# Interleaved instead of halved: which 128-row blocks make a quarter of w_down in a seven-product block multiply

## The chip, the cores and the metric

The kernel runs on one core of a Trainium2 chip. The metric is the device time of one execution in microseconds. The kernel before takes 941.87 us (median of 3 runs, 941.16 to 942.93).

## The reference, cut to what matters

One layer of a streaming encoder over 544 output tokens (512 prompt and 32 sample frames) with a model width of 1024. The change touches only the MLP at its end:

```python
def _mlp(x, g, w_up, w_down):          # w_up 1024 x 4096, w_down 4096 x 1024
    h = _rmsnorm(x, g)
    return jnp.square(jax.nn.relu(h @ w_up)) @ w_down
```

All is float32. The result must agree with float32 accuracy, so the kernel splits each operand into a rounded high part and the low rest and makes three matrix products of them (high x high, high x low, low x high).

## The kernel before, in words

Everything is done on one core with five engine programs written out by hand: SyncE loads weights, ScalarE (ACT) rounds them to the high part, GpSimd (POOL) makes the low part, TensorE (PE) multiplies, VectorE (DVE) and ACT empty the results. Order comes from each engine's own program order and from semaphores alone.

The hidden width of 4096 is taken in four rounds of 1024 (`rr`). In a round the kernel first makes eight tiles u[f], f = 0 to 7, of 128 hidden channels x 544 tokens ("up", PE line 659): tile f comes from one 512 KB block of 128 columns of w_up, loaded into one of the four slots of `w_raw`. Slot and order are those of `load_group` and of the loop at lines 512 to 521. Then the round's part of `@ w_down` is done. In the last round that is a plain multiply. In the first three (`rr < N_SEVEN`) it is a multiply of 2 x 2 blocks with seven products in place of eight (Winograd's form of Strassen's scheme, `seven`, PE line 981): for each of four pairs `p` of output tiles (`P_` = 4 rr + p, 12 in all) the 1024 x 256 piece of w_down is cut into quarters A11, A12, A21, A22. The first index is the output tile of the pair (a slot of `w_raw`), the second is one half of the 1024 hidden channels, which must be the same half of u that the forms B11, B21 and so on hold. Four sums of quarters (S1 to S4, `wsum_pair`, DVE line 1825) are made in `gate_c`.

Each of seven forms (A11, S1, A12, S2, S4, S3, A22, in this order on PE) is then made ready by these steps:

- ACT copies it, rounded, into its place in `w_hi` (line 1383). This waits until the product of the pair before that used the same place is done (`seven_free`).
- For the five forms in `BY_DMA` (A11, A12, A22 straight from `w_raw`; S4, S3 from `gate_c`) ACT also writes the negated rounded value into `w_lo` (line 1385), and POOL issues a DMA that adds the raw form onto it (line 635, `accum_op=ALU.add`). For S1 and S2 DVE subtracts (line 1842).
- PE waits for the low part (`low_made`), then makes 12 matmuls for the form.

A quarter is read through `quarter` (line 350). `w_raw[:, slot]` holds 8 blocks k of 128 values in each partition, one for each 128 hidden channels. Before the change a quarter's half h is the blocks 4h to 4h+3, one run of 512 values (2 KB) in a partition. To make it so that B11 and B21 pair channels m and m + 4, the tiles of w_up come in the order 0, 4, 1, 5, 2, 6, 3, 7.

The slots of `w_raw` are used again and again: a load of w_down for pair P_ (line 531) waits in `seven_left` until the low parts of pair P_ - 2 in that slot have landed and its sums are made; in pairs 2 and 3 of a round the next round's w_up loads (line 521) come behind the same wait.

Of the kernel before, what the change touches and what calls it, by code (L numbers as in the profile page):

```python
# [42 lines left out]
N_SEVEN = ROUNDS - 1  # L43
N_GROUPS = (3 + ROUNDS + 1) * GROUPS_PER_STAGE
PAIRS = KC // 2
# [43 lines left out]
def build(nc, x_prompt, x_sample, cache_k, cache_v, cache_conv, meta, g_mix, w_in, w_dw, b_dw,  # L89
# [5 lines left out]
    def weight(w, name):  # L95

        return w.rearrange("(k p) (n c) -> p k n c", p=P, c=P)
# [4 lines left out]
    wup_v = weight(w_up[0], "up")  # L102
# [12 lines left out]
    with ExitStack() as ctx:  # L115
        def sb(name, shape, dt=F32, where=ctx):
            return where.enter_context(nc.sbuf_tensor(name, shape, dt))

        def sem(name):
            return ctx.enter_context(nc.semaphore(name))  # L120


        w_raw = sb("w_raw", [P, RING, KC, P])
# [127 lines left out]
        raw_post = [sem(f"raw_post{n}") for n in range(4)]  # L251
# [64 lines left out]
        def lows_of_post(g, n):  # L316
            return RING * (g - 2) + n + 1
# [20 lines left out]
        def low_made(engine, P_, name):  # L338
            engine.wait_ge(wform_lo[MADE[name] - 1], (16 if name in BY_DMA else 1) * (P_ + 1))

        MADE = {w: n + 1 for n, (w, _, _, _) in enumerate(SEVEN)}

        ADDED = {"x11": 1, "z11": 2, "x12": 3, "y12": 4, "w12": 5, "x22": 6, "x21": 7, "y22": 8, "z21": 9}
# [6 lines left out]
        def quarter(P_, name):  # L350

            slot = 2 * (P_ % 2) + (name[1] == "2")
            h = int(name[2]) - 1
            return w_raw[:, slot, h * PAIRS:(h + 1) * PAIRS, :]

        def wsum(name):
            at = OUTTOK + SUM_FORMS.index(name) * PAIRS * P
# [2 lines left out]
        def raw_form(P_, name):  # L360
            return wsum(name) if name in SUM_FORMS else quarter(P_, name)
# [13 lines left out]
        def up_group(rr):  # L375
            return 3 * GROUPS_PER_STAGE + GROUPS_PER_STAGE * rr
# [32 lines left out]
        def x_half(t, h):  # L409
            (_, col, n), = X_COLS[t]  # L410
            return xT[:, h * KC // 2:(h + 1) * KC // 2, col:col + n]
# [5 lines left out]
        def _(sync):  # L417
# [70 lines left out]
            def load_group(g, view):  # L488
                for n in range(4):
                    sync.wait_ge(lo_post, lows_of_post(g - 1, n))  # L490
                    sync.dma_start(w_raw[:, n], view(n)).then_inc(raw_post[n], 16)
# [10 lines left out]
            def seven_left(P_, b):  # L502

                for name in ("A11", "A12") if b == 0 else ("A22",):
                    low_made(sync, P_, name)
                sync.wait_ge(wsum_done, len(SUM_FORMS) * (P_ + 1))

            for rr in range(ROUNDS):
                g0 = up_group(rr)
                if rr == 0:  # L510
                    with sync.Fori(0, 2) as j:
                        load_group(g0 + j, lambda n: wup_v[:, :, bass.ds(2 * j + n // 2 + PAIRS * (n % 2), 1), :].rearrange("p k n c -> p k (n c)"))
                else:
                    for j in range(2):
                        for n in range(4):
                            if j == 0:
                                seven_left(PAIRS * (rr - 1) + 2 + n // 2, n % 2)
                            sync.wait_ge(lo_post, lows_of_post(g0 + j - 1, n))

                            f = 4 * j + n if rr == N_SEVEN else 2 * j + n // 2 + PAIRS * (n % 2)  # L520
                            sync.dma_start(w_raw[:, n], wup_v[:, :, 8 * rr + f, :]).then_inc(raw_post[n], 16)
                if rr < N_SEVEN:
                    for p in range(PAIRS):
                        P_ = PAIRS * rr + p
                        for b in range(2):
                            slot = 2 * (p % 2) + b
                            if p < 2:
                                sync.wait_ge(lo_post, lows_of_post(g0 + 1, slot))
                            else:
                                seven_left(P_ - 2, b)  # L530
                            sync.dma_start(w_raw[:, slot], wdown_v[:, rr, :, 2 * p + b, :]).then_inc(raw_seven[slot], 16)
                else:
                    with sync.Fori(0, 2) as j:
                        load_group(g0 + 2 + j, lambda n: wdown_v[:, rr, :, bass.ds(4 * j + n, 1), :].rearrange("p k n c -> p k (n c)"))
# [115 lines left out]
        def _(pe):  # L650
# [63 lines left out]
            def scores(i, hh, first=False):  # L714
# [47 lines left out]
                for j in (2, 3):  # L762
                    bank, off, _, q0 = KT[j]
                    mm = score_split(bank, off, j, q0)
# [735 lines left out]
        def _(dve):  # L1500
# [313 lines left out]
            def wsum_pair(P_, name):  # L1814
                if name == "S1":
                    for slot in range(2 * (P_ % 2), 2 * (P_ % 2) + 2):
                        dve.wait_ge(raw_seven[slot], 16 * (P_ // 2 + 1))
                if P_:

                    low_made(dve, P_ - 1, name)  # L1820
                if name in ("S2", "S4"):
                    dve.wait_ge(wsum_done, len(SUM_FORMS) * P_ + SUM_FORMS.index(name))
                a, b, op = {"S1": (quarter(P_, "A21"), quarter(P_, "A22"), ALU.add), "S2": (wsum("S1"), quarter(P_, "A11"), ALU.subtract),
                            "S4": (quarter(P_, "A12"), wsum("S2"), ALU.subtract), "S3": (quarter(P_, "A11"), quarter(P_, "A21"), ALU.subtract)}[name]
                nc.vector.tensor_tensor(wsum(name), a, b, op).then_inc(wsum_done, 1)  # L1825
# [169 lines left out]
```

## Time and profile before

| | |
|---|---|
| median of 3 runs | 941.87 us |
| the profiled execution | 942.93 us |
| its span in the profile | 941.2 us |
| PE busy | 925.9 us (98%) |
| DVE, ACT, POOL busy | 648.1, 600.3, 250.5 us |
| mean granted TensorE clock | 0.996 |
| queue 0 (DMAs issued by POOL) | 16272 packets, 43.52 MB, 26.1% of 16 engines |
| queue 1 (DMAs issued by SP) | 176666 packets, 80.28 MB, 31.6% of 16 engines |

The span is the time between the first and the last instruction in the profile; the 1.7 us beside it are outside. Shares of DMA queues are the time that their packets took as a share of 16 engines' span, so the two can add up to a little more than 1 in a full stretch. "To landing" is the time from a DMA's issue to its semaphore.

### The profile page before, as it was taken

What the parts mean: (1) busy time and instruction counts of PE and PEld (TensorE: products, weight loads), DVE (VectorE), ACT (ScalarE), POOL (GpSimd) and SP (SyncE); (2) the same over time, 40 slices, a digit from 0 to 9 for tenths busy, and PEclk for the clock granted to TensorE, in tenths of its full rate; (3) what the DMA queues carried; (4) which work ended last, traced back from release to release, by engine and by line L of the source; (5) the groups of instructions that cost most, each with busy time, mean ns of one, the idle gap of its engine ahead of it and who ended that gap; (6) DMA issues with size and microseconds to landing.
All of it is one profiled execution on the core that took longest, in us unless ns stands there. A gap on an engine that the chain in (4) does not pass through costs nothing.

```text
span 941.2 us, 19528 instructions
## 1 busy us (share of the span) xinstructions
PE 925.9 (98%) x7329; PEld 906.3 (96%) x7329; DVE 648.1 (69%) x1181; ACT 600.3 (64%) x1004; POOL 250.5 (27%) x224
## 2 busy tenths in 40 slices
PE   8999999999999999999999999999999999999997
PEld 8999999999999999999999999989999999999997
DVE  6579999999999999998653335863587358622233
ACT  6787887878787878776833345663466356623353
POOL 5311010101010110102243444334433532444440
PEclk9999999999999999999999999999999999999998
DMA  7777667675758584859133232598259735963202
GB/s 183 159 171 135 172 126 178 119 183 108 180 113 187 104 199 98 173 133 211 46 112 90 85 85 78 120 211 186 68 119 224 172 89 113 230 155 88 87 23 96
DMA packets 198172, 127.25 MB, mean 135 GB/s; under 512 B 36397, under 2 KB 182237, under 8 KB 198122
## 3 DMA queue, kind: packets, MB, share of 16 engines
q1 hardware_dynamic: 176666, 80.28, 31.6%
q0 software_dynamic: 16272, 43.52, 26.1%
q10 hardware_dynamic: 5184, 2.78, 1.0%
q8 instruction: 32, 0.52, 0.2%
q14 instruction: 18, 0.15, 0.0%
HBM read 75.97 MB, written 7.06 MB: 88 GB/s over the span
## 4 chain that ended last, share of the span: by engine, by line
PE 84%; DVE 5%; ACT 4%; DMA 4%; SPq 1%; issue 1%; ACTq 0%; DVEq 0%
PE dense L659 61%; PE z L981 6%; PE dense L981 5%; PE z L779 3%; DMA w_lo<-w_raw 3%; PE dense L953 3%; PE z L743 2%; PE z L813 2%; DVE gate_c L1825 1%; ACT w_hi L1383 1%; DVE part L1782 1%; DVE acc L1559 1%; DMA w_raw<-in_w_in_dram 1%; ACT w_lo L1385 1%; ACT n L1346 1%
## 5 line engine op out<-in xcount | busy, mean ns | idle before, releaser
L659 PE MATMUL dense<-r_hi,w_hi 128*128 128x272 f32 (+1 forms) x1008 | 210.7, 291 | 1.4 <-ACT r_hi L1116 0.7
L659 PE MATMUL dense<-r_lo,w_hi 128*128 128x272 f32 (+1 forms) x1008 | 209.6, 289 | 0.0
L659 PE MATMUL dense<-r_hi,w_lo 128*128 128x272 f32 (+1 forms) x1008 | 209.5, 289 | 0.0
L630 POOL TENSOR_TENSOR w_lo<-w_raw,w_hi 128x1024 fp32r<-128x1024 f32 x56 | 134.8, 2410 | 196.9 <-ACT w_hi L1070 196.9
L1559 DVE SCALAR_TENSOR_TENSOR acc<-conv_in,cw_cur,acc 128x574 f32<-128x574 f32 x232 | 172.8, 811 | 0.5
L659 PEld LDWEIGHTS dense<-r_hi,w_hi 128*128 128x128 f32 x1008 | 158.2, 188 | 1.9 <-issue 0.9
L659 PEld LDWEIGHTS dense<-r_lo,w_hi 128*128 128x128 f32 x1008 | 158.7, 188 | 0.6 <-DVE r_lo L1540 0.6
L659 PEld LDWEIGHTS dense<-r_hi,w_lo 128*128 128x128 f32 x1008 | 159.0, 188 | 0.0
L607 POOL DMA_DIRECT2D w_lo<-w_raw x53 | 45.1, 851 | 361.9 <-ACT w_lo L1072 361.9
L1070 ACT ACTIVATE w_hi<-w_raw 128x1024 fp32r<-128x1024 f32 x110 | 115.7, 1052 | 34.1 <-PE z L981 21.6
L659 PE MATMUL dense<-s_hi,w_hi 128*128 128x272 f32 x640 | 132.2, 288 | 0.0
L659 PE MATMUL dense<-s_hi,w_lo 128*128 128x272 f32 x640 | 131.6, 288 | 0.0
L659 PE MATMUL dense<-s_lo,w_hi 128*128 128x272 f32 x640 | 131.4, 287 | 0.0
L659 PEld LDWEIGHTS dense<-s_lo,w_hi 128*128 128x128 f32 x640 | 100.0, 188 | 0.0
L659 PEld LDWEIGHTS dense<-s_hi,w_hi 128*128 128x128 f32 x640 | 99.7, 188 | 0.1
L659 PEld LDWEIGHTS dense<-s_hi,w_lo 128*128 128x128 f32 x640 | 99.7, 188 | 0.0
L1346 ACT ACTIVATE n<-n 128x544 f32<-128x544 f32 x32 | 21.1, 658 | 88.0 <-DVE n L1787 88.0
L1787 DVE SCALAR_TENSOR_TENSOR n<-dense,rstd 128x544 f32<-128x544 f32 x32 | 23.1, 723 | 69.2 <-PE dense L659 64.3
L1072 ACT ACTIVATE w_lo<-w_raw 128x1024 fp32r<-128x1024 f32 x53 | 55.6, 1050 | 0.0
L635 POOL DMA_DIRECT2D w_lo<-w_raw x36 | 30.6, 850 | 63.6 <-ACT w_lo L1385 62.7
L1383 ACT ACTIVATE w_hi<-gate_c 128x512 fp32r<-128x512 f32 x48 | 29.9, 629 | 16.9 <-DVE gate_c L1825 8.1
L1837 DVE TENSOR_TENSOR xT<-z,xT 128x272 f32<-128x272 f32 x48 | 19.8, 438 | 23.7 <-PE z L981 23.5
(305 smaller groups left out, 1941.9 us busy)
## 6 DMA issues: line engine op xcount, KB each, us to landing
w_raw<-in_w_in_dram SPq DMA_DIRECT2D x54, 512.0 KB, 5.7
w_lo<-w_raw POOLq DMA_DIRECT2D x53, 512.0 KB, 5.0
w_raw<-in_w_up_dram SPq DMA_DIRECT2D x32, 512.0 KB, 4.4
w_raw<-in_w_down_dram SPq DMA_DIRECT2D x32, 512.0 KB, 3.9
w_lo<-w_raw POOLq DMA_DIRECT2D x36, 256.0 KB, 5.6
w_lo<-gate_c POOLq DMA_DIRECT2D x24, 256.0 KB, 5.7
w_raw<-in_w_pw_dram SPq DMA_DIRECT2D x8, 512.0 KB, 3.9
w_raw<-in_w_out_dram SPq DMA_DIRECT2D x8, 512.0 KB, 3.9
```

What stands on the lines that cost most here:

```text
L607: pool.dma_start(w_lo[:, s].bitcast(F32), w_raw[:, s], accum_op=ALU.add).then_inc(lo_done[s], 16)
L630: pool.tensor_tensor(w_lo[:, n], w_raw[:, n], w_hi[:, n].bitcast(F32), ALU.subtract).then_inc(lo_post, 1)
L635: pool.dma_start(form_place(w_lo, name).bitcast(F32), raw_form(P_, name), accum_op=ALU.add).then_inc(wform_lo[MADE[name] - 1], 16)
L659: mm = nc.tensor.matmul(out[:, h, 0:half], w[:, wslot, k, :], m[:, k, c0 + h * half:c0 + (h + 1) * half], start=(k == 0 and n == 0), stop= ...
L779: mm = nc.tensor.matmul(z[:, dst[0], dst[1]:dst[1] + n], m[:], part_[src], start=False, stop=False, skip_group_check=True)
L953: mm = nc.tensor.matmul(part_out(n, p), w[:, n, k, :], m[:, k, cols], start=(k == 0 and j == 0), stop=(k == KC - 1 and j == 2))
L981: mm = nc.tensor.matmul(product_bank(P_, b), w[:, m, :], u_form(moving, m, low), start=(begin and m == 0 and j == 0), stop=(m == PAIRS - 1 ...
L1070: done = nc.scalar.activation(w_hi[:, s], w_raw[:, s], ACT.Copy)
L1072: done = nc.scalar.activation(w_lo[:, s], w_raw[:, s], ACT.Copy, scale=-1.0)
L1346: nc.scalar.activation(n32[:, n % 2, 0:OUTTOK], n32[:, n % 2, 0:OUTTOK], ACT.Square).then_inc(u32_done, 1)
L1383: mm = nc.scalar.activation(form_place(w_hi, name), raw_form(P_, name), ACT.Copy)
L1559: nc.vector.scalar_tensor_tensor(dst, src, w, dst, ALU.mult, ALU.add).then_inc(tap_done, 1)
```

## The change

```diff
         def quarter(P_, name):
 
             slot = 2 * (P_ % 2) + (name[1] == "2")
-            h = int(name[2]) - 1
-            return w_raw[:, slot, h * PAIRS:(h + 1) * PAIRS, :]
+            return w_raw[:, slot].rearrange("p (k t) c -> p t k c", t=2)[:, int(name[2]) - 1]
...
                 if rr == 0:
                     with sync.Fori(0, 2) as j:
-                        load_group(g0 + j, lambda n: wup_v[:, :, bass.ds(2 * j + n // 2 + PAIRS * (n % 2), 1), :].rearrange("p k n c -> p k (n c)"))
+                        load_group(g0 + j, lambda n: wup_v[:, :, bass.ds(4 * j + n, 1), :].rearrange("p k n c -> p k (n c)"))
...
-
-                            f = 4 * j + n if rr == N_SEVEN else 2 * j + n // 2 + PAIRS * (n % 2)
-                            sync.dma_start(w_raw[:, n], wup_v[:, :, 8 * rr + f, :]).then_inc(raw_post[n], 16)
+                            sync.dma_start(w_raw[:, n], wup_v[:, :, 8 * rr + 4 * j + n, :]).then_inc(raw_post[n], 16)
```

The tiles of w_up are now loaded in their natural order in every round, so that tiles 2m and 2m + 1 are a pair. A quarter of w_down is therefore every second block of 128 values: blocks 0, 2, 4, 6 for the first half and 1, 3, 5, 7 for the second. In a partition that is four runs of 512 bytes with gaps of 512 bytes in place of one run of 2 KB. The places in `w_hi` and `w_lo` and the sums in `gate_c` keep their layout. No instruction, wait or semaphore is added or taken away.

## Rows read from the trace of the kernel before

**Rows 1.** The page, busy time and share of TensorE.
```profile
PE 925.9 (98%) x7329; PEld 906.3 (96%) x7329; DVE 648.1 (69%) x1181; ACT 600.3 (64%) x1004; POOL 250.5 (27%) x224
```
**Rows 2.** Waits of PE: who for whom, us in total, times, longest.
```profile
PE dense L981 <- DMA w_lo<-w_raw: 4.2, 4, 2.2
...
PE dense L981 <- DVE xT L1835: 0.6, 1, 0.6
```
**Rows 3.** Windows: busy us of each engine, granted clock, DMA share, GB/s.
```profile
609.50:628.50 19.00, 16.80 (x121) 16.59 (x121) 12.79 (x28) 12.13 (x22) 7.74 (x10) 0.91 0.93 188
703.50:720.00 16.50, 15.37 (x119) 14.78 (x118) 13.03 (x28) 12.35 (x23) 8.09 (x10) 1.00 1.00 192
795.50:812.00 16.50, 15.30 (x118) 14.70 (x116) 12.90 (x28) 12.31 (x23) 8.19 (x10) 1.00 1.00 193
```
**Rows 4.** Chain of waits, first round: start us, us, what.
```profile
609.57 4.95 DMA w_lo<-w_raw
614.57 2.28 PE dense L981 x12
616.85 11.56 PE z L981 x84
628.41 10.54 PE dense L981 x84
```
**Rows 5.** Chain of waits, third round.
```profile
795.48 3.32 DMA w_lo<-w_raw
...
798.84 1.77 PE dense L981 x12
800.61 1.75 PE z L981 x12
...
803.89 8.11 DMA w_lo<-w_raw
...
812.13 10.78 PE dense L981 x84
```
**Rows 6.** Low-part DMAs of line 635: time to landing.
```profile
DMA to landing us min/median/max: 3.2/5.7/8.1
```
**Rows 7.** Groups by line: names, shapes, count, busy us, mean ns.
```profile
L1787 DVE SCALAR_TENSOR_TENSOR n<-dense,rstd 128x544 f32<-128x544 f32 x32 | 23.1, 723 | 69.2 <-PE dense L659 64.3 <-ACT rstd L1112 4.8
L1825 DVE TENSOR_TENSOR gate_c<-w_raw 128x512 f32<-128x512 f32 x24 | 16.5, 687 | 7.8 <-DMA w_raw<-in_w_down_dram 7.8
L1133 ACT ACTIVATE gate_a<-dense 128x544 f32<-128x544 f32 x8 | 5.0, 625 | 16.0 <-PE dense L659 16.0
L1383 ACT ACTIVATE w_hi<-w_raw 128x512 fp32r<-128x512 f32 x36 | 22.4, 623 | 10.7 <-PE dense L981 7.1 <-PE z L981 3.6
```
**Rows 8.** The page, POOL's own time for issuing a low-part DMA.
```profile
L607 POOL DMA_DIRECT2D w_lo<-w_raw x53 | 45.1, 851 | 361.9 <-ACT w_lo L1072 361.9
...
L635 POOL DMA_DIRECT2D w_lo<-w_raw x36 | 30.6, 850 | 63.6 <-ACT w_lo L1385 62.7
```
**Rows 9.** DMA queue of POOL, 785 to 788.5 us: packets, MB, share of 16 engines.
```profile
q0 software_dynamic: 144, 0.26, 43.5%
```
**Rows 10.** DMA queue of POOL, 100 to 200 us (rows of 4 KB).
```profile
q0 software_dynamic: 1788, 6.54, 36.1%
```
**Rows 11.** DMA queue of SP, 445 to 478 us (loads in pieces of 512 bytes).
```profile
q1 hardware_dynamic: 4981, 2.52, 26.6%
```
**Rows 12.** DMA queue of SP, 925 to 941 us (stores of 2 and 4 KB rows).
```profile
q1 hardware_dynamic: 768, 1.97, 33.6%
```
**Rows 13.** DMA queues and issues of POOL, 795.5 to 812 us.
```profile
q0 software_dynamic: 1131, 2.06, 76.3%
...
w_lo<-w_raw POOLq DMA_DIRECT2D x6, 256.0 KB, 5.5
```
**Rows 14.** Loads of w_up, issue to landing: 840 to 880, then 530 to 580.
```profile
w_raw<-in_w_up_dram SPq DMA_DIRECT2D x1, 512.0 KB, 4.2
...
w_raw<-in_w_up_dram SPq DMA_DIRECT2D x7, 512.0 KB, 4.0
```

## The prediction
> **What bounds the kernel now.** I read first the page's list of busy engines, then PE's waits, then the stretches with the seven products, then the DMA queues in them. PE is busy 98% of the span [rows 1], so a change pays or costs only through PE's gaps or clock. The reader should see three things. First, the touched stage has few gaps, nearly all of one kind: PE waits 4.2 us in four places for a low part built by DMA, and 0.6 us in a fifth place where the named DVE operation is not what came late [rows 2]. Second, the place of each gap is in the chain. In the first round the DMA for A22 of pair 0 is issued at 609.57 and takes 4.95 us, and PE starts again at 614.57; after this gap of 2.2 us the granted clock falls: 12 matmuls take 2.28 us and the next 84 take 11.56, where 84 take 10.54 elsewhere [rows 4, 5], and the window around has a mean clock of 0.91 [rows 3]. In the third round the same DMA takes 3.32 us and the gap is small, but the DMA for A11 of pair 2, issued at 803.89, takes 8.11 us and PE waits for it: pair 1 began at 800.61 and lasts 10.54, pair 2 begins at 812.13, some 0.9 us late [rows 5]. Third, why 8.11 us: from 795.5 to 812 the 16 DMA engines are full (share 1.00), as in the same stretch a round earlier, 703.5 to 720 [rows 3]. POOL's queue has 76% of it [rows 13]. So the low-part DMAs sit on PE's path in two ways: by their own length at pair 0, and by the queue's total at pair 2. This is where the change works.
>
> **The change part by part.** *Order of the w_up loads.* 24 loads are renamed among themselves, each still 1024 pieces of 512 bytes into the same slot behind the same waits. A load in natural order (last round) lands in 4.2 us, seven in the old order in 4.0 [rows 14]. Bound: 0.2 us either way on a load that PE doesn't wait for. I take 0.
>
> *DVE and ACT reading a quarter with gaps.* 48 sums on DVE and 72 copies on ACT now read four runs of 128 values. The nearest rows with more than one run are reads of two runs of 272: on DVE 723 ns for 544 columns against 687 for 512 (1.33 and 1.34 ns a column), on ACT 625 ns for 544 against 623 for 512 [rows 7]. So runs cost nothing that can be seen; I take 0. Both engines are idle a third of the span, but ACT's two copies of A22 stand on the path at pair 0; if each cost 20 ns more, three rounds would lose 0.1 us.
>
> *POOL's issue.* 36 of the 60 low-part DMAs read `w_raw`; these go from 128 rows of 2 KB to 512 pieces of 512 bytes on the reading side. POOL spends 850 ns on a DMA of 128 rows, whether of 4 KB or 2 KB [rows 8]. Both rows have 128 rows, so they don't say what four times as many pieces cost: from 0 to 3 x 0.85 = 2.55 us. I take 0, as the bytes at least cost nothing, and keep 2.55 for the range.
>
> *The DMA itself.* This is the term that counts. In a quiet stretch one 256 KB low-part DMA shows 144 packets, 128 rows and 16 for the semaphore, and 43.5% of 16 engines x 3.5 us = 24.4 us, which is 190 ns a row of 2 KB if the semaphore costs nothing [rows 9]. With 4 KB rows the same kind of DMA shows 6.54 MB = 1597 rows in 36.1% x 16 x 100 = 578 us, 362 ns a row [rows 10]. The slope is 172 ns for 2 KB, so of the 190 ns some 18 are fixed. A piece of 512 bytes is then 172/4 + 18 = 61 ns, four of them 244: 54 ns more for each old row, 128 rows over 16 engines are 8 on each, **+0.43 us per DMA**. Plain copies support a fixed part: 512-byte pieces take 26.6% x 16 x 33 / 4981 = 28 ns [rows 11], while SP's stores of 1.97 MB in 672 rows (768 packets less 16 for each of six DMAs) take 33.6% x 16 x 16 / 672 = 128 ns for 2930 bytes [rows 12]; that is 41 ns per 1000 bytes and 7 ns fixed. The bounds are wide. Below: if the fixed 18 ns belong to the semaphore packets, splitting is free, 0. Above: a piece may have a floor that longer rows hide; it can be as long as a whole row, 190 ns, which gives 4 x 190 - 190 = 570 ns a row and +4.6 us per DMA. I take 0.43 because slope and copies both point near it.
>
> The Trainium skill, page "DMA: Bandwidth & Descriptors", section "Why small descriptors are slow (HBM only)", says that transfers from SBUF to SBUF don't suffer from small descriptors, and its specification table puts the least size for full rate at 512 bytes, just what the pieces now have. By this rule the sum would be 0; the traces so far neither confirm nor refute it for an accumulating DMA.
>
> *From the DMA to PE.* At pair 0 PE stands behind A22's DMA in each of three rounds: 3 x 0.43 = 1.3 us, and in the first round A11's DMA of pair 1 runs beside it, another 0.4. In the full stretch up to A11 of pair 2, POOL issues six DMAs from `w_raw` [rows 13]; five (A22 of pair 0, A11, A12, A22 of pair 1, A11 of pair 2) must be through before PE goes on. With the engines full, five times 0.43 = 2.15 us are added to the gap, in rounds two and three: 4.3 us. In the first round pair 2 begins at 628.41 with no gap behind the 11.56 us of pair 1 [rows 4], so I count nothing. Other forms have a cushion: a form is rebuilt when its product has ended, so its DMA has 10.54 - 1.51 (own product) - 1.25 (two ACT copies) - 0.3 (hand-over) = 7.5 us [rows 4, 7] against a median of 5.7 [rows 6]; the queue is still full there, so I count 0.5 us for each of rounds two and three, 1.0. Then the clock: the gap before pair 2 grows from 0.9 to about 3 us, longer than the 2.2 us after which the clock fell in the first round, where it cost 0.5 (2.28 against 1.77) + 1.0 (11.56 against 10.54) = 1.5 us [rows 4, 5]. I count it for one of the two rounds. Sum: 1.3 + 0.4 + 4.3 + 1.0 + 1.5 = **8.5 us**. The profiled execution, 942.93 us (span 941.2 and 1.7 outside), becomes 951.4; it is the slowest of three, and on the median of 941.87 the same sum gives 950.4. I say 951.
>
> **The rivals.** *Splitting is free.* The cost is proportional to bytes, or the added time falls into cushions. For it: 18 ns is a small difference of two large numbers. Against it: the copies' 7 ns, and full engines where PE waits. It gives 0 to 1.9 us more, 942 to 943.8. It decides if a piece takes under some 48 ns. The rule of the Trainium skill cited above would have it so.
>
> *A floor under each piece.* The accumulate reads two streams and writes one, and what two long rows show need not hold for short ones; or POOL needs its time per piece. At 100 ns a piece a DMA gains 4 x 100 - 190 = 210 ns x 8 = 1.7 us. The stretch of pairs 1 to 3 is full already, so nearly all of it goes to PE: some 11 DMAs from `w_raw` a round x 1.7 less 2 us of cushion = 17 a round, 51 in all, 993 us. At 190 ns it would be 11 x 4.6 x 3 = 150 us, 1093. If POOL were to take 3.4 us an issue, a pair would need 3 x 3.4 + 2 x 0.85 = 11.9 us of it against 10.54 of PE, about +25 us, 967. Against a strong floor: 18 ns of fixed time at 2 KB leaves room only for one wholly hidden under the bytes.
>
> *Faster.* The load queue gets its turn between shorter packets: against a 61 ns piece in place of a 190 ns row, the loads of w_down in the full stretch (DVE waits 7.8 us for them [rows 7]) land sooner, forms are made sooner, and A11 of pair 2 lands in under 7.2 us in place of 8.11. At most PE's gaps of 4.8 us [rows 2] and the clock's 1.5 go: 942.9 - 6.3 = 936.6. Against it: A11 of pair 2 is issued late because PE's product before it ends at 802.36 [rows 5], not because a load is late, and less of the full engines for POOL's queue makes it later. It decides only if the pieces take no more engine time than the rows.
>
> **How the numbers follow.** The forecast (slower by 3 to 15 us) gets 0.50, free splitting 0.20, a floor 0.22, faster 0.08. A measurement of this kernel can't tell less than 0.2% (1.9 us) from no change. So faster 0.08, same 0.20, slower 0.72. The range runs from 941.5, which leaves out the faster case, to 985, which takes in a floor of up to about 95 ns a piece and leaves out the rest (0.12).
>
> **What would show it.** Right: in the profile after, POOL's queue has 36 x 384 = 13824 more packets with the same bytes, and in the quiet stretch one DMA from `w_raw` takes some 31 us of engine time in place of 24.4 and lands at 3.6 in place of 3.2 [rows 6, 9], while DMAs from `gate_c` keep theirs. The wait before pair 2 in rounds two and three is 2 to 3 us, with the clock below 1 behind it once or twice. DVE's 687 and ACT's 623 ns stay. Wrong: packets that don't grow in number (the pieces are joined), a piece clearly over 61 ns or at 48, POOL's 850 ns grown, or gaps of PE at other places, above all one before every product of pairs 1 to 3.

## The result, and the profile after

The changed kernel takes **950.87 us** (median of 4 runs, 949.6 to 952.47) against 942.4 us for the kernel before on the same chip (4 runs, 941.16 to 943.25). The ratio is **1.0092 [1.0072, 1.0112]**: 8.5 us slower. The profiled execution of the changed kernel is 950.32 us with a span of 948.6 us.

The page, busy time of the engines of the kernel after:

```profile
PE 928.7 (98%) x7329; PEld 907.5 (96%) x7329; DVE 648.1 (68%) x1181; ACT 600.2 (63%) x1004; POOL 266.2 (28%) x224
```

DVE and ACT have not moved by more than 0.1 us [rows 1]: their reads with gaps cost nothing. POOL has 15.7 us more. The groups by line (names, shapes, count, busy us, mean ns, idle before) say where; 1323 ns stand against 850 [rows 8], 686 against 687 and 623 against 623 [rows 7]:

```profile
L632 POOL DMA_DIRECT2D w_lo<-w_raw x36 | 46.1, 1323 | 60.7 <-ACT w_lo L1382 45.9 <-ACT w_hi L1380 14.3 <-issue 0.4
L1380 ACT ACTIVATE w_hi<-w_raw 128x512 fp32r<-128x512 f32 x36 | 22.4, 623 | 11.9 <-PE dense L978 6.7 <-PE z L978 5.1
L1822 DVE TENSOR_TENSOR gate_c<-w_raw 128x512 f32<-128x512 f32 x24 | 16.5, 686 | 11.0 <-DMA w_raw<-in_w_down_dram 11.0
```

(Lines of the kernel after are 3 lower than before: 632 for 635, 1380 for 1383, 978 for 981.) The waits of PE from 560 to 860 us, in the columns of [rows 2]:

```profile
PE dense L978 <- DMA w_lo<-w_raw: 3.4, 2, 2.2
PE z L978 <- DMA w_lo<-w_raw: 2.4, 4, 1.0
PE z L978 <- DVE xT L1834: 2.0, 3, 0.7
PE dense L978 <- DMA w_lo<-gate_c: 1.3, 2, 1.2
```

The sum goes from 4.8 us in five places to 9.1 us in eleven, and a kind is there that was not: PE waits for DVE's additions into xT at line 1834 (the 0.6 us of [rows 2] name another line). None of the eleven stands at the start of pair 2. POOL's DMA queue (q0) in two stretches: first a quiet one (693 to 699 us, which holds one cut DMA), and then in the full stretch of the third round (799.5 to 816.5 us): packets, MB, share of 16 engines.

```profile
q0 software_dynamic: 528, 0.26, 39.4%
...
q0 software_dynamic: 2640, 1.70, 79.7%
```

One cut DMA shows 528 packets, 512 pieces and 16 more, and 0.394 x 16 x 6 = 37.8 us of engine time where a whole one had 24.4 [rows 9]: 106 ns more for each old row, 0.85 us more on each engine. In the whole kernel q0 has 30096 packets for the same 43.52 MB, 13824 more. All 60 DMAs of the line take 4.1/6.5/8.4 us to landing (min/median/max) in place of 3.2/5.7/8.1 [rows 6].

The same two full stretches as windows (columns of [rows 3]):

```profile
704.00:721.00 17.00, 14.38 (x108) 13.56 (x108) 11.46 (x24) 11.52 (x21) 9.51 (x9) 1.00 1.09 173
799.50:816.50 17.00, 13.89 (x97) 13.20 (x95) 9.85 (x21) 10.22 (x19) 9.07 (x8) 0.90 1.04 163
```

The engines stay full (share over 1) but move 173 and 163 GB/s where they moved 192 and 193: more time for the same bytes. And in the third round the clock is 0.90 where it was 1.00.

The chain of waits in the third round shows which way the time reaches PE (start us, us, what):

```profile
800.20 4.38 DMA w_lo<-w_raw
...
804.60 8.25 DMA w_raw<-in_w_down_dram
...
812.93 0.70 DVE gate_c L1822
...
813.72 0.70 DVE gate_c L1822
...
814.94 0.43 DVE xT L1834
815.37 0.60 DVE gate_c L1822
815.97 0.36 DVE xT L1834
816.33 0.14 issue
816.47 3.25 PE z L978 x24
```

In the kernel before, the chain went from one low-part DMA to the next [rows 5]. Now it goes round the ring of slots: A22 of pair 0 lands and frees its slot of `w_raw`, the load of w_down for pair 2 goes into it and takes 8.25 us, DVE can then make the sums of pair 2, and in DVE's program these stand ahead of the additions of pair 1 that PE waits for.

Round by round (the first from its first product to the next up stage, the second and third from up stage to up stage) the two profiles give 46.2 and 46.0 us, 91.9 and 94.9, 92.1 and 95.3: -0.1, +3.0 and +3.2 us. The spans differ by 7.4 us; the other 1.3 us lie ahead of the touched stage. The -0.1 hides something: the clock fell in the first round of the profile before [rows 3, 4] and not in that of the kernel after. In e1 below, whose DMAs have whole rows as before and whose clock stayed at 1.00 there, the rounds take 44.9, 92.0 and 92.0 us. Against it the changed kernel loses 1.2, 3.0 and 3.3 us, 7.4 in all. That the median grew by 8.5 is not fully placed by these single executions.

### The profile page after: what moved, and what is told of

Read it like the earlier page. It is cut to its first block, busy times and chain, and to the rows that moved or that the text cites. A ratio compares the mean times of both kernels' runs of the same rounds, so it can differ in the third digit from the quotient of the medians.

```text
span 948.6 us, 19528 instructions
## 1 busy us (share of the span) xinstructions
PE 928.7 (98%) x7329; PEld 907.5 (96%) x7329; DVE 648.1 (68%) x1181; ACT 600.2 (63%) x1004; POOL 266.2 (28%) x224
## 3 DMA queue, kind: packets, MB, share of 16 engines
q0 software_dynamic: 30096, 43.52, 28.4%
## 4 chain that ended last, share of the span: by engine, by line
PE 80%; DMA 7%; DVE 6%; ACT 4%; issue 1%; SPq 1%; POOL 0%; DVEq 0%; ACTq 0%
PE dense L656 61%; PE z L978 4%; PE z L776 3%; DMA w_lo<-w_raw 3%; PE dense L978 3%; PE dense L950 3%; DMA w_raw<-in_w_down_dram 2%; PE z L740 2%; PE z L810 2%; DVE gate_c L1822 2%; ACT w_hi L1380 1%; DVE part L1779 1%; DVE acc L1556 1%; DMA x_tok<-in_x_sample_dram 1%; DMA w_raw<-in_w_in_dram 1%
## 5 line engine op out<-in xcount | busy, mean ns | idle before, releaser
L604 POOL DMA_DIRECT2D w_lo<-w_raw x53 | 45.1, 852 | 361.9 <-ACT w_lo L1069 361.9
L632 POOL DMA_DIRECT2D w_lo<-w_raw x36 | 46.1, 1323 | 60.7 <-ACT w_lo L1382 45.9
```

Of the source, the lines that this page charges most:

```text
L604: pool.dma_start(w_lo[:, s].bitcast(F32), w_raw[:, s], accum_op=ALU.add).then_inc(lo_done[s], 16)
L632: pool.dma_start(form_place(w_lo, name).bitcast(F32), raw_form(P_, name), accum_op=ALU.add).then_inc(wform_lo[MADE[name] - 1], 16)
```

## The experiments

Each ran beside the kernel before; ratios are to it, with their 95% interval. Diffs are cut: `...` marks lines left out, and where a DMA's `.then_inc(...)` is the same on both sides it is left out too. In e1, e4, e5 and e7 the forms hold other values than the reference's, so these serve for time alone. The medians of before were 942.43 us (e1, e4, e6, e7), 942.17 (e5, e8, e9, e10), 942.84 (e11 to e13) and 942.86 (e14).

**e1: all but the DMAs' rows.** The kernel after, with the source of the 36 DMAs one run of 2 KB.

```diff
-                    pool.dma_start(form_place(w_lo, name).bitcast(F32), raw_form(P_, name), accum_op=ALU.add)
+                    # raw: blocks 4h to 4h+3 for A11, A12, A22
+                    pool.dma_start(form_place(w_lo, name).bitcast(F32), raw, accum_op=ALU.add)
```

> The changed kernel, but the 36 low-part DMAs read the first or second 2 KB of the slot in one run, as before, and not the four interleaved runs; the low parts of A11, A12 and A22 are therefore those of other blocks and the output isn't the reference's. DVE and ACT still read four runs, w_up still comes in natural order. Theory (all of the 8.5 us comes from the cut rows of these DMAs): 942.4, ratio 1.000 within 0.002, POOL's issue back at 0.85 us and queue 0 back at 16272 packets. Rival (order of the loads, or DVE and ACT reading with gaps, costs something): clearly above, up to 950.9.

Measured: 942.63 us, 1.0002 [0.9992, 1.0012]. The whole cost is in the cut rows of these DMAs. The order of the w_up loads and the reads with gaps on DVE and ACT cost nothing that can be seen (together 1.1 us at most). POOL's issue is back at 851 ns.

**e4: only A22 of pair 0 whole** (3 of the 36 DMAs, the others cut).

```diff
+                    if name == "A22" and P_ % PAIRS == 0:
+                        h = int(name[2]) - 1
+                        raw = w_raw[:, 2 * (P_ % 2) + (name[1] == "2"), h * PAIRS:(h + 1) * PAIRS, :]
```

> The changed kernel, but the DMA for A22 of pair 0 (3 of the 36) reads one run of 2 KB per partition; its low part is that of other blocks. The quiet cut DMA takes about 0.85 us more engine time and 0.43 us more of POOL. Theory Q (full DMA engines: only total work counts): each round loses one of five or six additions, 0.85 x 2 rounds = 1.7 us, so about 949. Theory L (latency at pair 0: PE and the load ring of w_raw stand behind this one DMA): the whole of 3 x 1.3 us and more goes, 945 to 947.

Measured: 948.32 us, 1.0069 [1.0049, 1.0089]. Three whole DMAs give back 2.6 us, with an interval that reaches zero (1.0069 against 1.0092, each within 0.0020); the 33 others alone cost 5.9, with 4.6 to 8.4 by the interval of the ratio. Theory Q's 949 lies nearer than theory L's 945 to 947.

**e5: only A22 of pair 0 cut** (these 3, the 33 others whole; the diff is against e4).

```diff
-                    if name == "A22" and P_ % PAIRS == 0:
+                    if name not in SUM_FORMS and not (name == "A22" and P_ % PAIRS == 0):
```

> The complement of e4: the changed kernel, with cut rows only in the DMA for A22 of pair 0 (3 of 36); the other 33 DMAs from w_raw read one run of 2 KB, so their low parts are those of other blocks. Theory L (PE and the slot behind it wait for this one landing, 0.9 us later): +2.5 us against before, 944.9, so that e4 and e5 add up to the whole change. Theory Q (only work in the full queue counts): +0.85 in two rounds, 944.1 at most, and nothing in the first.

Measured: 948.04 us, 1.0054 [1.004, 1.0068]. Both theories (944.9 and 944.1) are passed. Three cut DMAs cost 5.9 us by the medians and 3.8 to 6.4 by the interval of the ratio, more than their own 3 x 0.85. So a cut DMA has no fixed price: these three cost more than 1.2 us each, the 33 of e4 under 0.3. That the two parts don't add up (5.9 and 5.9 against 8.5) is likely but not shown, since the interval of their sum overlaps that of the whole. The chain of e5 in the first round:

```profile
610.07 4.35 DMA w_lo<-w_raw
614.42 0.02 issue
614.43 9.23 DMA w_raw<-in_w_down_dram
623.66 0.03 DVEq L339
623.70 0.04 issue
623.74 0.70 DVE gate_c L1826
...
627.28 4.78 PE z L982 x24
```

It is the same ring. The load starts when A22 has landed and takes 9.23 us, where the kernel before has 6.6 for a load that starts at the same time (614.5). Why is not shown: in e5's second and third rounds the load behind A22 takes 5.5 us, less than the 5.7 of the kernel before. There the cut DMA itself is what costs: it lands in 4.22 us where 3.3 had been enough, and PE's gap is 1.5 us in place of 0.6.

A second thing makes the first round dear, the clock. The first round of the kernel before and of e5, as windows (columns of [rows 3]):

```profile
602.00:650.00 48.00, 45.80 (x353) 45.59 (x352) 30.35 (x65) 29.21 (x52) 20.09 (x20) 0.96 0.90 189
602.00:650.00 48.00, 43.65 (x323) 43.25 (x322) 28.10 (x60) 28.39 (x51) 17.45 (x19) 0.93 0.88 176
```

In e5 the clock falls twice, to 0.83 on average from 614.4 to 623.7 us, behind a gap of 2.24 us, and to 0.64 from 627.3 to 632.1, behind one of 2.10 us: the 24 matmuls of the chain's last line take 4.78 us where they take 3.24 otherwise. From busy time and clock I estimate 3.3 us for both falls, against 1.5 in the kernel before. So of the 3.8 us that e5's first round is longer, about half is waits and half is clock. The profiled execution is also the slowest of e5 (949.53 us; the fastest took 945.27).

**e6: POOL later, nothing cut.** The kernel before, with a small memset on POOL ahead of each of the 36 DMAs, about as long as the 0.43 us that a cut DMA adds to its issue.

```diff
+                    if name not in SUM_FORMS:
+                        pool.wait_ge(idled, idles)
+                        pool.memset(idle_col[:], 0.0).then_inc(idled, 1)
                     pool.dma_start(form_place(w_lo, name).bitcast(F32), raw_form(P_, name), accum_op=ALU.add)
```

> The kernel before, with a memset of 128x384 on POOL (about 0.42 us) ahead of each of the 36 DMAs that read w_raw, so that these are issued as much later as the changed kernel's are; rows stay whole. If issue time on POOL is an equal part of the 8.5 us: +3 to 4 us, 946. If the engine time of the pieces is what costs: at most the 3 x 0.4 us at pair 0, 943.7 or less, since full engines make the later issue invisible.

Measured: 943.12 us, 1.0007 [0.9997, 1.0018], at most 1.7 us, as the second theory had it. The memset takes 419 ns (median). The longer issue alone explains little.

**e7: two runs of 1 KB in place of four of 512 bytes.** The kernel before, with quarters of two blocks by turns (the halves of u keep their order, so the sums pair other channels than the reference has).

```diff
-            return w_raw[:, slot, h * PAIRS:(h + 1) * PAIRS, :]
+            return w_raw[:, slot].rearrange("p (a t b) c -> p t a b c", a=2, t=2)[:, h]
```

> The kernel before, with quarters that are interleaved by two blocks (blocks 0, 1, 4, 5 and 2, 3, 6, 7): two runs of 1 KB in a partition. The order of w_up stays that of before, so pairs of channels don't fit and the output isn't the reference's. With a fixed 31 ns per piece (from 296 ns for four pieces): 234 ns a row, +0.35 us engine time per DMA, POOL +0.14 us. If the cost is linear in pieces: a third of 8.5, 945.2. If cushions swallow the first part of it: 943 to 944.

Measured: 947.05 us, 1.0047 [1.0032, 1.0062]. Its queue in the quiet stretch from 693 to 699 us, then the durations of POOL's issues (min/median/max ns) in e7 and, below, in the kernel after:

```profile
q0 software_dynamic: 272, 0.26, 30.3%
...
L635 POOL DMA_DIRECT2D w_lo<-w_raw x36: 1182/1195/1721, 591.7 to 828.8; - x36
```

```profile
L632 POOL DMA_DIRECT2D w_lo<-w_raw x36: 1261/1276/1822, 592.5 to 832.1; - x36
```

0.303 x 16 x 6 = 29.1 us of engine time, 227 ns for each 2 KB row. With 190 for one run and 296 for four, a run more costs some 35 ns. So the engine time grows by the run, while POOL's issue makes a step for the first cut (848 to 1195 ns) and little after it (1276). The time of the kernel (+4.6 us for one more run a row, +8.5 for three) lies between the two laws and proves neither.

**e8 and e9: A22's low part by a subtraction on POOL**, with no DMA, in the kernel before (e8) and after (e9).

```diff
+                    if name in BY_POOL:          # ("A22",)
+                        pool.tensor_tensor(form_place(w_lo, name), raw_form(P_, name), form_place(w_hi, name).bitcast(F32), ALU.subtract)
+                        continue
```

> The kernel before, with the low part of A22 made by a subtraction on POOL in all 12 pairs (128x512, about 1.2 us by half of line 630's 2.4) in place of ACT's negated copy and the DMA. If the waits for these DMAs are what PE's gaps in the three rounds are made of, the gaps at pair 0 (2.2, 0.6, 0.6), the 1.5 us of clock behind the first and the 0.9 us before pair 2 in two rounds go: 936 to 937. Rival: POOL's reads slow DVE beside them (the 2.8 us of one sum beside a subtraction of POOL), and the gain is lost: 940 to 943.

> The changed kernel with the same edit as e8. Theory (the interleaved quarter is dear only for the DMA, at 35 ns of engine time per extra run, and only where the queue is full or PE stands behind): 24 cut DMAs are left, none at pair 0's A22 and four in the full stretch; most of the 8.5 us goes, 937 to 940. If the cost were spread over all 36 alike: a third goes, plus what e8 gains.

Measured: e8 944.57 us, 1.0027 [1.0018, 1.0036]; e9 943.87 us, 1.0022 [1.0012, 1.0032]. The expected gain of e8 is not there, and it is above the rival's 940 to 943 too; e9 meets neither of its numbers (937 to 940, or two thirds of the 8.5 us left). Its waits and its chain show a gap that moved to the first product of pair 1:

```profile
PE z L985 <- DMA w_lo<-w_raw: 6.3, 3, 2.2
```

```profile
608.81 1.58 POOL w_lo L637
610.39 5.43 DMA w_lo<-w_raw
615.82 0.04 issue
615.87 10.80 PE z L985 x84
```

POOL is busy for 1.58 us with the subtraction and issues A11 of pair 1 later, for which PE waits next. What counts is the comparison of the two: with twelve DMAs fewer the cut rows of the other 24 seem to cost nothing (e9 is not slower than e8). But both stand about 2 us at the start of pair 1 in every round, and that common gap can hide a cost; e14 looks behind it.

**e10: A11, A12 and A22 all on POOL**, in the kernel before.

```diff
-        BY_POOL = ("A22",)
+        BY_POOL = ("A11", "A12", "A22")
```

> The kernel before, with the low parts of A11, A12 and A22 all made by POOL's subtraction; of the DMAs only the 24 from gate_c are left. No form from w_raw touches a DMA, so the interleaving would cost nothing here. PE's gaps should be gone as in e8: 935 to 937. Rival: three subtractions of 1.2 us a pair beside DVE's work slow DVE, which then holds PE: 940 or more.

Measured: 951.48 us, 1.0095 [1.008, 1.011]. The expected gain turned into a loss. DVE's sums of e10, by line (in the kernel before these two groups have means of 687 and 1222 ns):

```profile
L1829 DVE TENSOR_TENSOR gate_c<-w_raw 128x512 f32<-128x512 f32 x24 | 24.7, 1030 | 0.0
L1829 DVE TENSOR_TENSOR gate_c<-gate_c,w_raw 128x512 f32<-128x512 f32 x12 | 17.4, 1448 | 0.9
```

The sums of the first group take 1030 ns on average here, the longest 3.42 us, with the subtractions of POOL beside them. (The kernel before has single sums of 2.8 us in its second group.) DVE is late with its additions, and PE waits for them (5.8 us in three places).

**e11: A22 of pair 0 two microseconds earlier**, in the kernel before. ACT makes it in the gap before T3 of the last tile of u; the place in `w_hi` is free by then.

```diff
                         for name in ("T2", "T3", "T4"):
+                            if name == "T3" and f == KC - 1:
+                                form_high(PAIRS * rr, "A22")
                             u_sum_high(rr, m, name)
...
-                    form_high(P_, "A22")
```

> The kernel before, but ACT makes the high and negated copy of A22 of pair 0 before the sum T3 of the last tile of u, in place of after T4, so POOL can issue its DMA some 2 us earlier (607.4 in place of 609.6 in the first round). Nothing else moves; the number of DMAs and their rows stay. Theory (the landing of A22 of pair 0 is what costs at pair 0, and the load of w_down behind it): PE's gaps there (2.2, 0.6, 0.6 us) and the 1.5 us of lower clock in the first round go, 942.2 - 4.9 = 937.3 us. Rival (the work only waits at the next place, as when POOL did the subtraction, 944.6): 941 to 943 us.

Measured: **937.8 us, 0.9956 [0.9943, 0.9969]**, expected 937.3. By the medians that is 5.0 us less than before, by the ratio 4.1 (2.9 to 5.4). It beats both kernels. Of PE's 4.8 us of waits 1.5 are left, none at pair 0:

```profile
PE z L981 <- DMA w_lo<-w_raw: 1.5, 2, 0.9
```

**e12: the same edit in the kernel after.**

> The kernel after, with the same edit: A22 of pair 0 is made some 2 us earlier; all 36 DMAs still read four runs a row. Theory (the ring: A22's landing, then the load of w_down for pair 2 into its slot, then DVE's sums, then PE): an earlier landing pulls the whole ring forward, so most of the 8.5 us go, 943 to 945 us (943.9 was measured with A22 made by POOL without a DMA). Rival (the cost is in the sheer engine time of the 33 other DMAs, in the full stretch): only the gap at pair 0 goes, 948 us.

Measured: 946.58 us, 1.0047 [1.0028, 1.0065]. The edit gives 4.3 us here too, but the cost of the cut rows stays: 946.58 against 937.8 is 8.8 us. So a late A22 of pair 0 is not the cause of the 8.5 us; the theory asked for 943 to 945, the rival for 948, and the interval (945.5 to 949.0) holds the rival's number alone. The chain of e12 in the second round:

```profile
709.44 8.23 DMA w_lo<-w_raw
717.69 8.54 DMA w_raw<-in_w_down_dram
726.31 0.70 DVE gate_c L1823
727.10 0.63 DVE gate_c L1823
729.84 3.24 PE dense L978 x24
```

The ring is there again, one pair further on: low part of pair 1, load of pair 3, DVE's sums, PE in pair 2. Both transfers in it run among full engines. Whichever pair it enters by, the ring has two long transfers, and among cut rows both are longer. The load behind A22 of pair 0 takes 6.6, 5.7 and 5.7 us in the three rounds before, 5.5, 5.7 and 5.7 in e1, and 7.1, 7.3 and 8.2 in the kernel after.

**e13: DVE's sums later.** The kernel after, with pair 1 taking pair 0's order on DVE: x12 stands behind one sum of the late load, not behind three operations on it.

```diff
-                if p > 0:
+                if p > 1:
                     made(P_, "A11")
...
                 else:
+                    if p:
+                        made(P_, "A11")
+                        add_product(P_, "x11")
                     following("S1")
...
-                if p == 0:
+                if p <= 1:
                     following("S2")
```

> The kernel after, but in pair 1 of a round DVE takes its steps in the order of pair 0: the additions of x11, then S1 of the next pair, then z11, x12 and y12, and only then the sums S2, S4, S3 of the next pair and S1's low part. So what PE waits for (x12) stands behind one sum of the late load and not behind three. Theory: the waits of PE for DVE's x12 (2.0 us in three places) go, 950.9 - 2.0 = 948.9 us, while the waits for DMAs stay. Rival (the later sums make S4's and S3's DMAs of the next pair late): 951 to 954 us, with waits of PE for DMAs from gate_c.

Measured: 950.31 us, 1.0084 [1.0071, 1.0097]. The waits of PE in e13:

```profile
PE dense L978 <- DMA w_lo<-w_raw: 6.3, 6, 2.2
PE z L978 <- DMA w_lo<-w_raw: 1.4, 2, 0.7
PE dense L978 <- DVE xT L1832: 0.9, 1, 0.9
PE dense L978 <- DMA w_lo<-gate_c: 0.9, 2, 0.7
```

PE no longer waits for line 1834 (2.0 us), yet the sum of its waits is 9.5 us in place of 9.1: what DVE no longer holds up, the low-part DMAs do. DVE's order is where the delay shows, not where it comes from. The theory's 948.9 lies outside the interval (949.5 to 952.0), and the waits of PE for DMAs from `gate_c` that the rival asked for did not grow (0.9 us, 1.3 in the kernel after).

**e14: e9 and e12 together.** The kernel after, A22 on POOL and made early (the two diffs above).

> e9 (the kernel after, A22's low part by a subtraction on POOL) and e12's edit together: A22 of pair 0 is made some 2 us earlier, so POOL's subtraction is done before A11 of pair 1 is ready. In e8 and e9 PE stood 2.2 us at the start of pair 1 in each round, and this common gap may have hidden what the 24 remaining cut DMAs cost. Theory (cut rows cost only where the DMA engines have no room, and 12 DMAs fewer leave room): the gaps of 5.7 us at pair 1 go and nothing takes their place, 943.9 - 5.7 = 938.2 us, as e11 (937.8). Rival (the common gap hid the cost of the cut rows): a good part stays as waits for low parts or for DVE behind late loads, 941 to 944 us.

Measured: 941.77 us, 0.9989 [0.998, 0.9998]. PE's waits of e14:

```profile
PE dense L982 <- DMA w_lo<-w_raw: 1.5, 1, 1.5
PE z L982 <- DVE xT L1839: 1.1, 2, 0.6
PE dense L982 <- DVE xT L1837: 1.1, 2, 0.6
PE z L982 <- DMA w_lo<-w_raw: 0.7, 1, 0.7
```

The gap at pair 1 is gone (5.7 us before), but 4.4 us of others stand in its place: the rival's number is met. It is 4.0 us above e11, the whole-row kernel with an early A22, against 8.8 us for e12. So with 12 of the 36 cut DMAs gone more than half of the difference is gone. How much of the remaining 4.0 us belongs to the other 24 is not known: some may come from the subtractions on POOL (a DVE sum takes 787 ns here on average, not 687, though 684 in e9), and the control, whole rows with A22 on POOL and early, was not run. Nor does the comparison price cut rows alone, since the twelve DMAs went with their bytes. DVE does not wait for a load of w_down in e14 (10.8 us in e12), and the DMA share from 690 to 730 and from 782 to 822 us is 0.95 and 0.93, in e12 0.98 and 0.97.

## Why the prediction was right, step by step

The direction, the place and the size came out: 951.0 was said, 950.87 measured. The steps did so in part only.

- *The w_up loads' order, DVE and ACT with gaps: 0.* Right; e1 shows all three at once.
- *POOL's issue: 0 taken, 2.55 us kept as the upper end.* Wrong in size: +0.43 us (median 848 to 1276 ns; mean 850 to 1323). e6 prices it in PE's time at 1.7 us or less. The rival's 25 us for an issue of 3.4 us don't follow from its own numbers either: 12 pairs x (11.9 - 10.54) are 16.
- *The DMA: +0.43 us of engine time each.* Mis-sized by half: +0.85 us. The kind of law was right, a fixed part for each run, but 18 ns from the slope between 2 and 4 KB rows were too few; it is some 35 ns, and a piece takes 74 ns, not 61. The mistake was to take a fixed time from a small difference of two windows, and to let plain copies (7 ns) count as support.
- *Splitting is free* fell for this DMA, in which SBUF is both source and target and the engine accumulates: 24.4 us of engine time became 37.8 with pieces of 512 bytes, and 29.1 with 1 KB. The Trainium skill, page "DMA: Bandwidth & Descriptors", section "Why small descriptors are slow (HBM only)", says that transfers from SBUF to SBUF don't suffer from small descriptors; the measurement differs, and it decides for this DMA. Plain copies between places of SBUF were not measured here.
- *A floor under each piece* of 100 or 190 ns fell: a piece takes 296 / 4 = 74 ns.
- *Faster, since loads get turns between shorter packets:* fell. The load behind A22 of pair 0 took longer among cut rows in every round (7.1, 7.3 and 8.2 us, against 6.6, 5.7 and 5.7). The 9.23 us of this load among whole rows, in e5's first round, stand alone: it took 5.5 us in e5's other two.
- *From the DMA to PE.* Predicted for the rounds: 0.8, 3.1 and 3.1 us, and 1.5 for the clock in one of the last two. The profiles show -0.1 (1.2 against e1), +3.0 and +3.2, the last with the clock at 0.90 inside it (an estimate from busy time and clock is 1.7 us of its 3.2). With 0.85 us a DMA the prediction's own sum, five DMAs on the path in a full stretch, would have come to some 14 us. So two mistakes met: the term was half as large as it should be, and the sum let every one of the five DMAs pass on its whole growth. The rounds grew by 3.0 and 3.2 us where five times 0.85 are 4.3. In the first round the gap of 2.2 us came in smaller parts (the longest 1.23 us), and the clock stayed at 1.00 where it had been 0.91 [rows 3].
- *The clock.* The prediction tied its fall to a gap above 2.2 us. In the third round it did fall behind a gap of 2.21 us, but in e1 a gap of 2.44 us was followed by no fall. So the 1.5 us in the sum came out partly by luck, and when the clock falls stays open.
- *The place.* The prediction had PE wait at A11 of pair 2, for its low part, 2 to 3 us in rounds two and three. PE waited there not at all. Its gaps stood in pair 0 (2.21 us at A22 in the third round), at the start of pairs 1 and 3, and late in pair 1 behind DVE. By the prediction's own signs of being wrong, three came: a piece clearly over 61 ns, POOL's 850 ns grown, and gaps at other places. What it did not price is the ring: low part lands, load of w_down, DVE's sums, DVE's additions, PE. It had these waits in view (7.8 us on DVE [rows 7]), as a gain only. They grew to 11.0 us.

So the total is right by compensation, and its nearness to 950.87 is luck. Shown by the runs: the cost is in the cut rows of these DMAs (e1), the later issue on POOL is a small part of it at most (e6), it is no fixed price for each DMA (e4 and e5), and it isn't tied to A22 of pair 0 being late (e12) nor to DVE's order (e13). Argued only: that the room on the DMA engines is what decides (the shares go that way, and no run changed it alone), and how much of the 8.5 us goes through the low parts themselves, how much through the loads behind them, and how much through the clock. No run held one of them still.

## What to carry to other kernels

Before a layout is changed, count the runs in a partition that each DMA reads: a compute engine read four runs at no cost, while an accumulating DMA paid for each of them on the DMA engines and once on the issuing engine. The price differed from place to place (e4, e5), so look at what waits behind each transfer, and follow the slot that a DMA frees to the load behind it. Don't multiply the price of one DMA by their number (five times 0.85 us would have been too much); and a gap at the head of such a stretch may be had cheaper by making its first operand earlier (e11: 4 to 5 us for one moved line) than by any change of the transfer.

## What the runs showed of the hardware

- An accumulating SBUF to SBUF DMA took 190, 227 and 296 ns of engine time for 2 KB in one, two and four runs: some 35 ns a run more.
- POOL's issue of such a DMA of 128 rows took 848, 1195 and 1276 ns for one, two and four runs a row: a step, then little.
- Beside POOL's subtractions of 128x512 (1.3 to 1.8 us each) DVE's sums of the same size grew from 687 to 1030 ns on average, the longest to 3.42 us (e10, 36 subtractions). With 12 subtractions the mean was 684 (e9), 705 (e8) and 787 ns (e14).
- DVE and ACT read 128x512 float32 in four runs of 128 in the same time as in one: 686 against 687 ns, 623 against 623.
- A load of 512 KB that took about 4 us in a quiet stretch [rows 14] took 5.4 to 8.4 us beside the low-part DMAs in the seven-product stretches of the kernel before, and up to 9.1 us in those of the kernel after.
- The granted clock fell behind gaps of TensorE of 2.20 us (before), 2.21 us (after), 2.24 and 2.10 us (e5), and did not behind one of 2.44 us (e1).
